# Two perceptron-heavy blocks in fp32: who makes the remainders of the down-projection weights

## The chip, the cores and the metric

One core of a Trainium2 chip runs the whole program. The metric is the device time of one execution in microseconds; the times below are of the kernel before the change.

## The reference

Two transformer blocks run one after the other on one sequence of 512 tokens and width 1024, all in fp32. The first has a recurrent mixer, differential attention, a memory cross-attention and a perceptron; the second has two layers, a gated linear attention and a sliding-window attention, each followed by a perceptron. The three perceptrons all have this form (their weights are 1024 x 4096 and 4096 x 1024):

```python
def sq_relu_mlp(h, w_up, w_down):
    u = jax.nn.relu(h @ w_up)
    return (u * u) @ w_down
```

TensorE gets fp32 accuracy from three products of rounded operands: each weight block w is split into hi = w rounded to the matrix format and lo = w - hi, each activation likewise, and w x is taken as hi x_hi + lo x_hi + hi x_lo.

## The kernel before, in words

Weights stream through in blocks of 1 MB, numbered by n over the whole program. Block n lies in slot n % 4 of `raw` (the SBUF tile that loads fill); SP issues the loads in order (`load_mlp`, L1359), each when `raw_free` says that the slot's last user is done. ScalarE rounds a block into its hi tile (`hi`, L2014, the activation at L2021). For plain blocks VectorE makes the remainder (`lo`, the subtraction at L2399). In the perceptrons lo is written over the raw weights: `raw_lo` and `raw` are two names for the same bytes.

A perceptron has 32 blocks, in an order written out in `mlp_order` (L115): up blocks U(g, b) make two of the 16 chunks of hidden activations, down blocks D(g, b) add a product of four chunks' worth of rows onto half of the output. The order is U(0,0), U(0,1), U(1,0), D(0,0), U(1,1), D(0,1), and then up and down in turn. So i = 0, 1, 2 are up blocks done with plain chunks of 24 matmuls (`chunk`); i = 3 is the first down block; from i = 4 on even i are up blocks done by a scheme of seven block products (`up_fast`, L1597 for its matmuls, 84 of 256 columns each), odd i are down blocks (`down`, 48 matmuls of 512 columns), and i = 30 and 31 are down blocks again. In the third perceptron the last two down blocks are not run by `down` but by `last_chunk`, half the tokens at a time. There are 16 down blocks in each perceptron, 48 in all.

TensorE runs the blocks in that order and waits at the head of each one in `block_ready` for its remainder. ScalarE's order is written out by hand in its `mlp` (L2104): near the head of a perceptron it rounds block n + 3 behind the squares of block n + 1 (`square(n + 1, 1)`), then block n + 5 behind the activations of block n + 2. In the loop over i = 4, 6, .. 28 it takes four snapshots of the running up block out of PSUM (`snap`), rounds the sums of the next up block (`group_hi`) and rounds the down block n + i + 3; then come `square_pair` and `pair_hi`, which square and round the activations just made. At i = 28 it rounds block n + 30 between the first and the second snapshot. VectorE's `mlp` (L2540) calls `lo` for one down block in each turn. GpSimd issues small loads and does additions (`fold_acc`, L1468) between the perceptrons; during them it waits.

`DONE`, `STD_NO` and `FAST` are tables that say which value a semaphore has once a block is done; `wide` views a block as four rows of 512 columns, which is how down blocks are laid out.

Of the kernel before, what the change touches and what calls it, by code (L numbers as in the profile page):

```python
# [19 lines left out]
P = 128  # L20
T = 512
D = 1024
# [22 lines left out]
CONST, _c = {}, 0  # L45
# [64 lines left out]
          ("SOA", 2, 4, (0, 1)), ("SOB", 2, 4, ANY), ("MLP3", 32, 2, WOB_RING)]  # L110
FIRST, ACC, DONE = {}, [], []
FAST, STD_NO, MLP_AT, HI_FREE = {}, [], {}, []


def mlp_order(last):  # L115
# [10 lines left out]
for _name, _count, _chunks, _ring in STAGES:  # L126
    FIRST[_name] = len(ACC)
    for _i in range(_count):
        ACC.append(len(ACC_BANK))
        DONE.append(_done)  # L130
        STD_NO.append(len(ACC) - 1 - len(FAST))
        HI_FREE.append(len(ACC) - 3)
        if _name[:3] == "MLP":
            _n = len(ACC) - 1
            _nth = int(_name[3]) - 1
            _kind, _g, _b = mlp_order(_nth == 2)[_i]
            MLP_AT[_n] = (_nth, _i, _kind, _g, _b)
            HI_FREE[_n] = _n - (2 if _i < 2 else 3)
            if _kind == "U" and _i >= 4:
                FAST[_n] = len(FAST)  # L140
                continue
            _chunks = 4 if _kind == "D" else 2
            if _nth == 2 and _i >= 30:
                continue
        _done += _chunks
        for _c in range(_chunks):
            _k = len(ACC_BANK)
            _b = _ring[_k % len(_ring)]
            ACC_BANK.append(_b)
            ACC_NEED.append(_last.get(_b, 0))  # L150
            _last[_b] = _k + 1
# [2 lines left out]
ACC.append(len(ACC_BANK))  # L154
DONE.append(_done)
STD_NO.append(N_END - len(FAST))


PRODUCTS = dict(P1=(4, 0, 3), P2=(6, 1, 0), P6=(2, 5, 3), P5=(1, 3, 2), P7=(0, 4, 3), P4=(5, 6, 1), P3=(3, 2, 2))
# [71 lines left out]
def program(nc, A, out):  # L231
# [2 lines left out]
    ds = bass.ds  # L234
    ctx = ExitStack()
    with ctx:
        sem_names = """ld_const ld_vec ld_small ld_lora ld_x0 ld_x1 ld_x2 ld_x3 ld_x4 ld_x5 ld_x6 ld_x7 ld_mem ld_kv st_kv0 st_kv1 kv_hi kv_lo ld_gk ld_bias0 ld_bias1 ld_bias2 ld_rel st_bias st_out
            w_hi_ready w_lo_ready acc_done acc_evac vec_ready bias_mm bias_ev ld_w0 half_hi half_lo
            norm_sq norm_add norm_ss norm_ln norm_rstd x_hi x_lo h_final
            fold_sq fold_add fold_ss fold_step  # L240
            mn_sq mn_add mn_step mx_hi mx_lo
# [300 lines left out]
        def rwkv_pe(pe, mm, wait, fill):  # L542
# [54 lines left out]
            for st, hp in RW_OPS["p"]:  # L597
# [9 lines left out]
                if (st, hp) in entry:  # L607
                    wait(*entry[(st, hp)])
                if st == "zw":
                    wait("ld_lora", 48)  # L610
                    wait("rw_lora", 1)
                    last = mm(bank[:], lora[0:64, fs], p_rw[0:64, 12, :], start=True, stop=True)
                elif st == "za":
# [368 lines left out]
        def gla_pe(pe, mm, wait, chunk, blocks, block_tm, norm_stat, chunk_tokens):  # L982
# [3 lines left out]
            mm(X[2][:], C("ones"), fold_acc[:], start=True, stop=True).then_inc(S["fold_ss"], 1)  # L986
            chunk(N_GQK, 0, g_hi, g_lo_)
            wait("acc_evac", ACC[N_GQK])
            wait("ld_gk", 64)
            wait("fold_step", 5)  # L990
            for c in range(4):
                r = slice(32 * c, 32 * c + GLR)
# [336 lines left out]
        def _(sp):  # L1329
            def raw_free(n):  # L1330

                if n >= 4 and n - 4 in FAST:
                    sp.wait_ge(S["st_mm"], 7 * FAST[n - 4] + PRODUCT_NO["P4"])
                elif n >= 4 and n - 4 in MLP_AT:
                    sp.wait_ge(S["acc_done"], DONE[n - 3])
                elif n >= 4:
                    sp.wait_ge(S["w_lo_ready"], STD_NO[n - 4] + 1)

            def load(n, src, cols=BW):

# [76 lines left out]

        @block.gpsimd
        def _(pool):
            for i, name in enumerate(("lam_q1", "lam_q2")):  # L1420
                pool.dma_start(lamv[i:i + 1, 0, :], A[name]).then_inc(S["ld_small"], 16)
            for i, name in enumerate(("lam_k1", "lam_k2")):
# [2 lines left out]
            pool.wait_ge(S["x_lo"], KT)  # L1425
            pool.wait_ge(S["norm_sq"], KT)
            pool.dma_start(memT[:], A["mem"]).then_inc(S["ld_mem"], 16)
            pool.dma_start(lora[0:64, :], A["w_decay_up"][0]).then_inc(S["ld_lora"], 16)
            pool.dma_start(lora[64:128, :], A["a_up"][0]).then_inc(S["ld_lora"], 16)
            pool.dma_start(g_up[:], A["g_up"][0]).then_inc(S["ld_lora"], 16)  # L1430

            pool.wait_ge(S["ld_vec"], 16)
            for k in range(14):
# [21 lines left out]
            pool.dma_start(vf[:].rearrange("p t (b n) -> p (t b) n", b=4), kv_rows[:, 8:16, :]).then_inc(S["ld_kv"], 16)  # L1455
            pool.wait_ge(S["acc_evac"], ACC[N_MQ] + 1)
            pool.wait_ge(S["norm_ss"], 2)
            pool.dma_start(onehot[:], A["onehot"]).then_inc(S["ld_rel"], 16)
            pool.dma_start(relx[0:32, :], A["rel_table_2"]).then_inc(S["ld_rel"], 16)
            pool.dma_start(relx[32:33, :], A["consts"][0:1, CONST["ones"][0]:CONST["ones"][0] + 16]).then_inc(S["ld_rel"], 16)  # L1460
            pool.wait_ge(S["bias_ev"], 1)
            pool.dma_start(bias_rows, biasrow[:].unsqueeze(1).to_broadcast([16, P, 384])).then_inc(S["st_bias"], 16)
            pool.wait_ge(S["st_bias"], 16)
            for c in range(1, KT):
                pool.wait_ge(S["fold_sq"], c + 1)
                if c > 1:
                    pool.wait_ge(S["fold_add"], c - 1)
                nc.gpsimd.tensor_tensor(fold_acc[:], (ut[0] if c == 1 else fold_acc)[:], ut[c % 2][:], ALU.add).then_inc(S["fold_add"], 1)  # L1468
            pool.wait_ge(S["acc_evac"], ACC[N_GLR])
            for c in range(4):  # L1470
                pool.dma_start(w_gk2[32 * c:32 * c + GLR, :], A["a_w_gk2_2"][0][:, c * P:c * P + P]).then_inc(S["ld_gk"], 16)
            pool.wait_ge(S["acc_evac"], ACC[N_KV])
            for c in range(3):
                pool.dma_start(bias[c][:], bias_skewed(c)).then_inc(S[f"ld_bias{c}"], 16)
# [4 lines left out]
            for c in range(KT):  # L1479
                if c + 3 < KT:  # L1480
                    pool.wait_ge(S["sw_s"], 4 * (c + 1))
                    pool.dma_start(bias[c % 3][:], bias_skewed(c + 3)).then_inc(S[f"ld_bias{c % 3}"], 16)
                pool.wait_ge(S["sw_rd"], c + 1)
                r_ = sw_small[c % 2][4]
                s_ = sc[c % 3][:, 0, :, P:256]
                nc.gpsimd.tensor_tensor(s_, s_, r_[:, 0:2].unsqueeze(2).to_broadcast([P, 2, P]), ALU.mult)
                s_ = sc[c % 3][:, 1:4].rearrange("p a b n -> p (a b) n")
                nc.gpsimd.tensor_tensor(s_, s_, r_[:, 2:8].unsqueeze(2).to_broadcast([P, 6, 256]),
                                        ALU.mult).then_inc(S["sw_p"], 1)


        @block.tensor
        def _(pe):
# [9 lines left out]
                return M[ACC_BANK[k]]  # L1503

            def block_ready(n):
                pe.wait_ge(S["w_lo_ready"], STD_NO[n] + 1)

            def exact3(dst, wh, wl, xh, xl, start, stop):
                mm(dst, wh, xh, start=start, stop=False)  # L1509
# [303 lines left out]
            def mem_transposes(hd):  # L1813
                wait("ma_p", hd + 1)
                if hd:
                    wait("ma_pt_lo", 2 * hd)
                else:
                    wait("bias_ev", 1)
                for t in range(2):
                    for qb in range(4):  # L1820
                        last = nc.tensor.transpose(X[2 + t][:, qb * P:qb * P + P], me[hd % 2][:, qb, t * P:t * P + P],
                                                   C("ident"))
                    last.then_inc(S["ma_tr"], 1)
# [19 lines left out]
            chunk(N_MQ + 1, 1, x2_hi, x2_lo)  # L1843
            chunk(N_MQ + 2, 0, x2_hi, x2_lo)
            mem_scores(1)
            wait("ld_rel", 48)
            mm(X[3][0:16, 0:384], relx[:], onehot[:], start=True, stop=True).then_inc(S["bias_mm"], 1)
            chunk(N_MQ + 2, 1, x2_hi, x2_lo)
            mem_transposes(0)
            chunk(N_MQ + 3, 0, x2_hi, x2_lo)  # L1850
# [162 lines left out]
        def _(act):  # L2013
            def hi(n):  # L2014

                slot_free(act, n)
                arrived(act, n)
                if n == N_GLR:
                    nc.scalar.activation(copies(hi_of(n)), copies_of(raw[:, n % 4]), ACT.Copy).then_inc(S["w_hi_ready"], 1)
                else:  # L2020
                    nc.scalar.activation(hi_of(n)[:, :, :], raw[:, n % 4], ACT.Copy).then_inc(S["w_hi_ready"], 1)  # L2021

            def norm_chunk(i, c, src, ready=None, x=None, tok=T, sem=("norm_sq", "norm_add", "x_hi")):

# [253 lines left out]
            hi(N_MQ + 3)  # L2278
            query_hi(4)
            mem_exps(1)  # L2280
            act.wait_ge(S["bias_mm"], 1)
            nc.scalar.activation(biasrow[:], X[3][0:16, 0:384], ACT.Copy).then_inc(S["bias_ev"], 1)
            query_hi(5)
            hi(N_MOA)
            mem_pt_hi(0)
# [104 lines left out]
        def _(dve):  # L2390
# [149 lines left out]
            def mlp(n, nth, rstd_of, i_, j_, fname, foff, wname=None, woff=0, hi_=None, lo_=None):  # L2540
# [37 lines left out]
                up_out(n + 1, 0)  # L2578
                comb_lo(nth, 2)
                up_out(n + 1, 1)  # L2580
                lo(n + 3)
                pair_lo(n + 1)
                comb(nth, 3, fname, foff)
                up_out(n + 2, 0)
# [8 lines left out]
                add(3, 0, 1, 2)  # L2593
                for i in range(4, 30, 2):
                    add(i - 1, 3)
                    lo(n + i + 1)
                    if i < 28:
                        sums(i + 2)
                        group_lo(n + i + 2, 0)
                        group_lo(n + i + 2, 1)  # L2600
                    up_even(n + i)
                    up_odd(n + i)
                    if i < 28:
                        group_lo(n + i + 2, 2)
                        group_lo(n + i + 2, 3)
                    else:
                        lo(n + 30)
                    if nth < 2 or i < 28:
                        if i % 4 == 0:
                            add(i + 1, 0)  # L2610
                        pair_lo(n + i)
                        add(i + 1, *range(1 if i % 4 == 0 else 0, 3))
                if nth == 2:
                    pair_lo(n + 28)
                    lo(n + 31)
                    final(29)
                    norm_step(i_, 3, j_, h[:, 3, :], gain(3), lo_, hi_)
                    return
                add(29, 3)
                lo(n + 31)  # L2620
                final(30)
                lo(n + 32)
                final(31)
# [380 lines left out]
```

## Time and profile before

| | us |
|---|---|
| three runs | 1935.07, 1935.68, 1937.64 |
| median | 1935.68 |
| span of the profiled execution | 1937.4 |
| TensorE busy in it | 1912.2 |
| VectorE busy in it | 1333.0 |
| ScalarE busy in it | 837.4 |
| GpSimd busy in it | 121.1 |

The span runs from the first to the last instruction of one profiled execution. TensorE's matmuls overlap in its pipeline, so the durations in single rows are longer than the distance from one matmul's start to the next one's; the distance is what a stream of them costs. PE is TensorE, PEld its weight loads, DVE is VectorE, ACT ScalarE, POOL GpSimd, SP the engine that issues most loads.

### The profile page before, as it was taken

Reading aid. Unit: us, or ns where it says so; the run is one execution under the profiler, and the core shown is the slowest. Engines: PE = TensorE matmul, PEld = TensorE weight load, DVE = VectorE, ACT = ScalarE, POOL = GpSimd, SP = SyncE. Lnnn points to the kernel's source line nnn. Section 1 sums busy time; section 2 is a strip of 40 time slices with the busy share of each in tenths; the row PEclk is TensorE's granted clock in tenths of the full one; section 3 lists DMA queues with packets and bytes.
Section 4 is the critical chain, followed back from the end, with each engine's and each line's share of the span. In section 5 each row is a group of like instructions: output and inputs, shape, how many; then the busy total and the mean of one; then the engine's idle time right before and its main releaser. Section 6 shows DMA issues by size and latency. Waiting matters only on the chain.

```text
span 1937.4 us, 32713 instructions
## 1 busy us (share of the span) xinstructions
PE 1912.2 (99%) x14002; PEld 1646.6 (85%) x14002; DVE 1333.0 (69%) x1755; ACT 837.4 (43%) x1254; POOL 121.1 (6%) x130
## 2 busy tenths in 40 slices
PE   8999999999999999999999999999999999999998
PEld 6877898888788898887989889889987788898897
DVE  5576869576677777767545687767677768777665
ACT  4333744344354344344224443434444645344342
POOL 1055100000000000010000000000002300000000
PEclk9999999999999999999999999999999999999999
DMA  8221402237123233224220233323342113233231
GB/s 271 88 66 66 137 10 80 88 132 128 46 89 108 87 110 109 88 78 140 90 87 23 66 98 98 109 87 109 102 144 88 50 47 106 90 106 109 87 109 44
DMA packets 138831, 182.62 MB, mean 94 GB/s; under 512 B 4917, under 2 KB 103429, under 8 KB 138304
## 3 DMA queue, kind: packets, MB, share of 16 engines
q1 hardware_dynamic: 135392, 168.91, 26.9%
q0 software_dynamic: 3296, 11.63, 2.9%
q8 instruction: 111, 1.82, 0.4%
q14 instruction: 32, 0.26, 0.0%
HBM read 172.66 MB, written 7.34 MB: 93 GB/s over the span
## 4 chain that ended last, share of the span: by engine, by line
PE 94%; DVE 3%; ACT 1%; issue 1%; DMA 0%; SPq 0%; DVEq 0%; ACTq 0%
PE X L1597 20%; PE M L1509 19%; PE M L1510 19%; PE M L1511 19%; PE X L643 3%; PE M L1570 1%; PE M L1571 1%; PE M L1572 1%; PE M L1925 1%; PE X L1902 1%; PE X L1913 1%; PE X L1780 1%; PE X L1749 1%; DMA raw<-in_w_in_dram 0%; PE X L1511 0%
## 5 line engine op out<-in xcount | busy, mean ns | idle before, releaser
L1510 PE MATMUL M<-u,raw_lo 128*128 128x512 f32 x728 | 287.9, 396 | 0.0
L1509 PE MATMUL M<-u,w_hi 128*128 128x512 f32 x728 | 287.9, 395 | 0.0
L1511 PE MATMUL M<-u,w_hi 128*128 128x512 f32 x728 | 286.1, 393 | 0.0
L2021 ACT ACTIVATE w_hi<-raw 128x2048 fp32r<-128x2048 f32 x113 | 215.6, 1908 | 93.5 <-PE M L1511 47.9
L2076 ACT ACTIVATE us<-X 128x256 f32<-128x256 f32 x156 | 60.2, 386 | 426.9 <-PE X L1597 426.9
L2549 DVE TENSOR_TENSOR h<-h,M 128x512 f32<-128x512 f32 x184 | 123.7, 685 | 144.7 <-PE M L1511 144.6
L1597 PE MATMUL X<-t,w_hi 128*128 128x256 f32 x936 | 173.2, 282 | 0.0
L1511 PEld LDWEIGHTS M<-u,w_hi 128*128 128x128 f32 x728 | 137.6, 189 | 32.8
L1509 PEld LDWEIGHTS M<-u,w_hi 128*128 128x128 f32 x728 | 136.8, 188 | 30.8
L1510 PEld LDWEIGHTS M<-u,raw_lo 128*128 128x128 f32 x728 | 136.7, 188 | 29.8
L2399 DVE TENSOR_TENSOR raw_lo<-raw,w_hi 128x2048 fp32r<-128x2048 f32 x57 | 130.3, 2287 | 23.7 <-ACT w_hi L2021 23.7
L1597 PEld LDWEIGHTS X<-t,w_hi 128*128 128x128 f32 x936 | 146.4, 188 | 0.0
L2399 DVE TENSOR_TENSOR w_lo<-raw,w_hi 128x2048 fp32r<-128x2048 f32 x52 | 118.9, 2289 | 29.9 <-ACT w_hi L2021 29.9
L1597 PE MATMUL X<-t,w_lo 128*128 128x256 f32 x468 | 131.7, 281 | 0.0
L1597 PE MATMUL X<-f,wx 128*128 128x256 f32 x624 | 117.8, 282 | 0.0
L1597 PEld LDWEIGHTS X<-f,wx 128*128 128x128 f32 x624 | 98.6, 189 | 1.7
L2480 DVE TENSOR_TENSOR w_lo<-w_sum,w_hi 128x1024 fp32r<-128x1024 f32 x78 | 91.9, 1220 | 0.0
L1597 PEld LDWEIGHTS X<-t,w_lo 128*128 128x128 f32 x468 | 88.2, 188 | 0.0
L1597 PE MATMUL X<-f,raw_lo 128*128 128x256 f32 x312 | 87.9, 282 | 0.0
L1509 PE MATMUL M<-gx_hi,w_hi 128*128 128x512 f32 (+2 forms) x232 | 85.1, 367 | 1.0 <-DVE w_lo L2399 0.5
L1511 PE MATMUL M<-gx_lo,w_hi 128*128 128x512 f32 (+2 forms) x232 | 84.3, 363 | 0.0
L1510 PE MATMUL M<-gx_hi,w_lo 128*128 128x512 f32 (+2 forms) x232 | 84.3, 363 | 0.0
(525 smaller groups left out, 4542.2 us busy)
## 6 DMA issues: line engine op xcount, KB each, us to landing
raw<-in_w_up_dram SPq DMA_DIRECT2D x48, 1024.0 KB, 5.4
raw<-in_w_down_dram SPq DMA_DIRECT2D x48, 1024.0 KB, 5.0
raw<-in_w_in_dram SPq DMA_DIRECT2D x12, 1024.0 KB, 8.6
raw<-in_a_w_in_dram SPq DMA_DIRECT2D x12, 1024.0 KB, 5.3
h<-in_x_dram SPq DMA_DIRECT2D x16, 256.0 KB, 4.8
raw<-in_w_mk_dram SPq DMA_DIRECT2D x4, 1024.0 KB, 4.9
raw<-in_w_mv_dram SPq DMA_DIRECT2D x4, 1024.0 KB, 5.2
raw<-in_w_out_dram SPq DMA_DIRECT2D x4, 1024.0 KB, 5.1
```

The lines of the kernel that those rows point to most:

```text
L643: last = mm(blk(bank, hh, cp, cpar), a_, b_, start=True, stop=True)
L1509: mm(dst, wh, xh, start=start, stop=False)
L1510: mm(dst, wl, xh, start=False, stop=False)
L1511: return mm(dst, wh, xl, start=False, stop=stop)
L1570: mm(o_, hi[:, kt, ts_], w_hi[:, n % 2, kt, cs], start=kt == 0, stop=False)
L1571: mm(o_, hi[:, kt, ts_], w_lo[:, n % 2, kt, cs], start=False, stop=False)
L1597: last = mm(region(r), (wl if p_ == 1 else wh)[:, m, :], xl if p_ == 2 else xh, start=name in ("P1", "P2", "P4", "P5") and m == 0 and p_ = ...
L2021: nc.scalar.activation(hi_of(n)[:, :, :], raw[:, n % 4], ACT.Copy).then_inc(S["w_hi_ready"], 1)
L2076: nc.scalar.activation(at_, region(r), ACT.Copy).then_inc(S["st_snap"], 1)
L2399: TTO(lo_of(n)[:, :, :], raw[:, n % 4], hi_of(n)[:, :, :].bitcast(f32), ALU.subtract).then_inc(S["w_lo_ready"], 1)
L2480: TTO(to_, from_, hi_.bitcast(f32), ALU.subtract).then_inc(S["st_lo"], 1)
L2549: TTO(h[:, 4 * b + c, :], h[:, 4 * b + c, :], acc(n + i, c), ALU.add).then_inc(S["acc_evac"], 1)
```

## The change

The down blocks' remainders are made without VectorE. ScalarE rounds the block into its hi tile as before and then writes the negated rounded weights over the raw ones (`raw_lo` = -hi, in place). GpSimd waits for that and issues a transfer that reads the same raw weights once more from memory and adds them onto what lies there: -hi + w = lo. TensorE waits at the head of a down block for this transfer's semaphore (two, taken in turn) instead of VectorE's. VectorE's 16 calls of `lo` for down blocks are gone from each perceptron; `LO_NO` numbers the remainders that VectorE still makes. GpSimd's transfers of a perceptron are three loops: for the first one behind the store of the bias table, for the second behind the four loads of `w_gk2`, for the third at the end of its program. Some semaphores for small tables are merged to make room for the new names.

```diff
+DOWN, LO_NO = {}, []
...
+        LO_NO.append(STD_NO[-1] - len(DOWN))
...
+            if _kind == "D":
+                DOWN[_n] = len(DOWN)
...
                 elif n >= 4:
-                    sp.wait_ge(S["w_lo_ready"], STD_NO[n - 4] + 1)
+                    sp.wait_ge(S["w_lo_ready"], LO_NO[n - 4] + 1)
...
+            def remainders(first):
+
+                _, down = mlps[first]
+                for n in range(first, first + 32):
+                    if n in DOWN:
+                        k, (_, _, _, g, b) = DOWN[n], MLP_AT[n]
+                        pool.wait_ge(S["down_neg"], k + 1)
+                        if k >= 2:
+                            pool.wait_ge(S["acc_done"], DONE[DOWN_AT[k - 2]] + 1)
+                        pool.dma_start(wide(raw_lo[:, n % 4]), down[:, 4 * g:4 * g + 4, 512 * b:512 * b + 512],
+                                       accum_op=ALU.add).then_inc(S[f"down_lo{k % 2}"], 16)
...
             pool.wait_ge(S["st_bias"], 16)
+            remainders(N_MLP1)
             for c in range(1, KT):
                 pool.wait_ge(S["fold_sq"], c + 1)
...
+            remainders(N_MLP2)
             pool.wait_ge(S["acc_evac"], ACC[N_KV])
...
+            remainders(N_MLP3)
...
             def block_ready(n):
-                pe.wait_ge(S["w_lo_ready"], STD_NO[n] + 1)
+                if n in DOWN:
+                    wait(f"down_lo{DOWN[n] % 2}", 16 * (DOWN[n] // 2 + 1))
+                else:
+                    wait("w_lo_ready", LO_NO[n] + 1)
...
                     nc.scalar.activation(hi_of(n)[:, :, :], raw[:, n % 4], ACT.Copy).then_inc(S["w_hi_ready"], 1)
+                if n in DOWN:
+                    nc.scalar.activation(raw_lo[:, n % 4], raw[:, n % 4], ACT.Copy, scale=-1.0).then_inc(S["down_neg"], 1)
...
                 up_out(n + 1, 1)
-                lo(n + 3)
                 pair_lo(n + 1)
...
                 for i in range(4, 30, 2):
                     add(i - 1, 3)
-                    lo(n + i + 1)
...
-                    else:
-                        lo(n + 30)
...
-                    lo(n + 31)
```

## Rows read from the trace of the kernel before

**Rows 1.** The page: busy time by engine, and the chain that ended last, by engine.
```profile
PE 1912.2 (99%) x14002; PEld 1646.6 (85%) x14002; DVE 1333.0 (69%) x1755; ACT 837.4 (43%) x1254; POOL 121.1 (6%) x130
...
PE 94%; DVE 3%; ACT 1%; issue 1%; DMA 0%; SPq 0%; DVEq 0%; ACTq 0%
```

**Rows 2.** Busy time by stretch (us, engines, granted clock, DMA): middle of perceptron one.
```profile
571.00:835.00 264.00, 264.00 (x1669) 238.38 (x1668) 189.89 (x213) 108.62 (x138) 0.00 (x0) 1.00 0.31 100
```

**Rows 3.** Waits of TensorE's weight loads: us in total, times, longest.
```profile
PEld M L1509 <- DVE w_lo L2399: 1.7, 2, 1.0
```

**Rows 4.** Line 2399, VectorE's remainders: count, ns min/median/max, first and last start.
```profile
L2399 DVE TENSOR_TENSOR raw_lo<-raw,w_hi x57: 2284/2285/2294, 518.4 to 1899.4; 128x2048 fp32r<-128x2048 f32 x57
```

**Rows 5.** Timeline of ScalarE (start us, us): rounding of each first down block.
```profile
554.28 1.90 ACT L2021 ACTIVATE w_hi<-raw 128x2048 fp32r<-128x2048 f32 x1
...
1120.93 1.90 ACT L2021 ACTIVATE w_hi<-raw 128x2048 fp32r<-128x2048 f32 x1
...
1612.77 1.90 ACT L2021 ACTIVATE w_hi<-raw 128x2048 fp32r<-128x2048 f32 x1
```

**Rows 6.** Perceptron three, i = 28: ScalarE's timeline; chain: TensorE's seven products.
```profile
1885.37 1.91 ACT L2021 ACTIVATE w_hi<-raw 128x2048 fp32r<-128x2048 f32 x1
...
1883.56 10.01 PE X L1597 x84
```

**Rows 7.** Timeline of TensorE: first matmuls of the three first down blocks.
```profile
559.85 0.40 PE L1509 MATMUL M<-u,w_hi 128*128 128x512 f32 x1
560.09 0.40 PE L1510 MATMUL M<-u,raw_lo 128*128 128x512 f32 x1
...
1126.90 0.40 PE L1509 MATMUL M<-u,w_hi 128*128 128x512 f32 x1
...
1618.29 0.40 PE L1509 MATMUL M<-u,w_hi 128*128 128x512 f32 x1
```

**Rows 8.** Timelines: rounding and first matmul of i = 13 and i = 5.
```profile
645.45 1.91 ACT L2021 ACTIVATE w_hi<-raw 128x2048 fp32r<-128x2048 f32 x1
...
665.60 0.39 PE L1509 MATMUL M<-u,w_hi 128*128 128x512 f32 x1
...
569.58 1.90 ACT L2021 ACTIVATE w_hi<-raw 128x2048 fp32r<-128x2048 f32 x1
...
581.01 0.40 PE L1509 MATMUL M<-u,w_hi 128*128 128x512 f32 x1
```

**Rows 9.** Timelines: rounding and first use of the very last down block.
```profile
1897.50 1.90 ACT L2021 ACTIVATE w_hi<-raw 128x2048 fp32r<-128x2048 f32 x1
...
1906.01 0.28 PE L1509 MATMUL X<-u,w_hi 128*128 128x256 f32 x1
```

**Rows 10.** Timelines of GpSimd and SP; transfers (KB each, median us to landing).
```profile
388.05 0.55 POOL L1454 DMA_DIRECT2D kf_mem<-kv_rows  x1 [77.03 <-DVE p_rw L979]
388.59 0.55 POOL L1455 DMA_DIRECT2D vf_mem<-kv_rows  x1
...
391.10 0.37 SPq L1342 DMA_DIRECT2D raw<-in_w_mq_dram  x1
...
kf_mem<-kv_rows POOLq DMA_DIRECT2D x1, 1024.0 KB, 5.2
vf_mem<-kv_rows POOLq DMA_DIRECT2D x1, 1024.0 KB, 7.2
...
bias_rows<-biasrow POOLq DMA_DIRECT2D x1, 3072.0 KB, 33.3
```

**Rows 11.** Timeline of SP at perceptron one's first down block.
```profile
560.04 0.37 SPq L1342 DMA_DIRECT2D raw<-in_w_up_dram  x1
```

**Rows 12.** TensorE's first and eleventh matmul; last stretch by engine and granted clock.
```profile
7.87 0.76 PE L1509 MATMUL M<-xm_hi,w_hi 128*128 128x512 f32 x1 [7.87 <-DVE xm_lo L2638]
...
12.28 0.49 PE L1510 MATMUL M<-xm_hi,w_lo 128*128 128x512 f32 x1
...
1932.00:1937.00 5.00, 0.00 (x0) 0.00 (x0) 2.57 (x7) 0.00 (x0) 0.00 (x0) 0.50 0.63 210
```

More of the change, by code:

```diff
@@ L156 @@
 STD_NO.append(N_END - len(FAST))
+LO_NO.append(STD_NO[-1] - len(DOWN))
+DOWN_AT = list(DOWN)
 PRODUCTS = dict(P1=(4, 0, 3), P2=(6, 1, 0), P6=(2, 5, 3), P5=(1, 3, 2), P7=(0, 4, 3), P4=(5, 6, 1), P3=(3, 2, 2))
@@ L236, in program @@
     with ctx:
-        sem_names = """ld_const ld_vec ld_small ld_lora ld_x0 ld_x1 ld_x2 ld_x3 ld_x4 ld_x5 ld_x6 ld_x7 ld_mem ld_kv st_kv0 st_kv1 kv_hi kv_lo ld_gk ld_bias0 ld_bias1 ld_bias2 ld_rel st_bias st_out
-            w_hi_ready w_lo_ready acc_done acc_evac vec_ready bias_mm bias_ev ld_w0 half_hi half_lo
+        sem_names = """ld_const ld_vec ld_small ld_tables ld_x0 ld_x1 ld_x2 ld_x3 ld_x4 ld_x5 ld_x6 ld_x7 ld_mem ld_kv st_kv0 st_kv1 kv_hi kv_lo down_neg down_lo0 down_lo1 ld_bias0 ld_bias1 ld_bias2 st_bias st_out
+            w_hi_ready w_lo_ready acc_done acc_evac vec_ready bias_step ld_w0 half_hi half_lo
             norm_sq norm_add norm_ss norm_ln norm_rstd x_hi x_lo h_final
@@ L609, in rwkv_pe @@
                 if st == "zw":
-                    wait("ld_lora", 48)
+                    wait("ld_tables", 48)
                     wait("rw_lora", 1)
@@ L988, in gla_pe @@
             wait("acc_evac", ACC[N_GQK])
-            wait("ld_gk", 64)
+            wait("ld_tables", 160)
             wait("fold_step", 5)
@@ L1427, in _ @@
             pool.dma_start(memT[:], A["mem"]).then_inc(S["ld_mem"], 16)
-            pool.dma_start(lora[0:64, :], A["w_decay_up"][0]).then_inc(S["ld_lora"], 16)
-            pool.dma_start(lora[64:128, :], A["a_up"][0]).then_inc(S["ld_lora"], 16)
-            pool.dma_start(g_up[:], A["g_up"][0]).then_inc(S["ld_lora"], 16)
+            pool.dma_start(lora[0:64, :], A["w_decay_up"][0]).then_inc(S["ld_tables"], 16)
+            pool.dma_start(lora[64:128, :], A["a_up"][0]).then_inc(S["ld_tables"], 16)
+            pool.dma_start(g_up[:], A["g_up"][0]).then_inc(S["ld_tables"], 16)
             pool.wait_ge(S["ld_vec"], 16)
@@ L1457, in _ @@
             pool.wait_ge(S["norm_ss"], 2)
[L1458 to L1461, printed above, removed]
+            pool.dma_start(onehot[:], A["onehot"]).then_inc(S["ld_tables"], 16)
+            pool.dma_start(relx[0:32, :], A["rel_table_2"]).then_inc(S["ld_tables"], 16)
+            pool.dma_start(relx[32:33, :], A["consts"][0:1, CONST["ones"][0]:CONST["ones"][0] + 16]).then_inc(S["ld_tables"], 16)
+            pool.wait_ge(S["bias_step"], 2)
             pool.dma_start(bias_rows, biasrow[:].unsqueeze(1).to_broadcast([16, P, 384])).then_inc(S["st_bias"], 16)
             pool.wait_ge(S["st_bias"], 16)
+            remainders(N_MLP1)
             for c in range(1, KT):
@@ L1470, in _ @@
             for c in range(4):
-                pool.dma_start(w_gk2[32 * c:32 * c + GLR, :], A["a_w_gk2_2"][0][:, c * P:c * P + P]).then_inc(S["ld_gk"], 16)
+                pool.dma_start(w_gk2[32 * c:32 * c + GLR, :], A["a_w_gk2_2"][0][:, c * P:c * P + P]).then_inc(S["ld_tables"], 16)
+            remainders(N_MLP2)
             pool.wait_ge(S["acc_evac"], ACC[N_KV])
@@ L1817, in mem_transposes @@
                 else:
-                    wait("bias_ev", 1)
+                    wait("bias_step", 2)
                 for t in range(2):
@@ L1845, in _ @@
             mem_scores(1)
-            wait("ld_rel", 48)
-            mm(X[3][0:16, 0:384], relx[:], onehot[:], start=True, stop=True).then_inc(S["bias_mm"], 1)
+            wait("ld_tables", 96)
+            mm(X[3][0:16, 0:384], relx[:], onehot[:], start=True, stop=True).then_inc(S["bias_step"], 1)
             chunk(N_MQ + 2, 1, x2_hi, x2_lo)
@@ L2280, in _ @@
             mem_exps(1)
-            act.wait_ge(S["bias_mm"], 1)
-            nc.scalar.activation(biasrow[:], X[3][0:16, 0:384], ACT.Copy).then_inc(S["bias_ev"], 1)
+            act.wait_ge(S["bias_step"], 1)
+            nc.scalar.activation(biasrow[:], X[3][0:16, 0:384], ACT.Copy).then_inc(S["bias_step"], 1)
             query_hi(5)
@@ L2619, in mlp @@
                 add(29, 3)
-                lo(n + 31)
                 final(30)
```

## The prediction

> **What bounds the kernel now.** I read the page first: busy time by engine and the chain that ended last. TensorE is busy for 1912.2 us of a span of 1937.4 us, and 94% of the chain is TensorE work; VectorE, which the change relieves, is busy for 69% [rows 1]. Then the table by stretches, for the middle of a perceptron, where most of the removed work lies: TensorE is busy for 264.00 of 264 us there, at a granted clock of 1.00 [rows 2]. Then the waits: in the whole execution TensorE's weight loads wait 1.7 us, twice, for the line that makes remainders, and the tile named there is w_lo, which no perceptron's down block uses [rows 3]. So VectorE's subtraction of a down block costs TensorE nothing today. It is off the path, and taking it away can give nothing back by itself. What remains is to see whether the new way to the same tile is ready in time at each of the 48 down blocks. For that I read the timeline of ScalarE and of TensorE round the first, a middle and the last down block of a perceptron, and the GpSimd transfers for a price.
>
> **What is removed.** 48 subtractions of 2.285 us [rows 4], 109.7 us of VectorE time, all beside a busy TensorE: gain 0 (at most the 1.7 us of waits above, and those belong to other blocks). VectorE's next steps (pair_lo, comb, add) come up to 2.3 us earlier; TensorE waits for none of them, so nothing follows. The renamed and merged semaphores wait for the same events: 0.
>
> **What is added on ScalarE.** Behind each down block's rounding stands a second copy of the same size, taken as 1.9 us like the rounding [rows 5]; 48 of them are 91 us on an engine that is busy for 43% [rows 1]. Queued behind it are square_pair and pair_hi (the squared activations), which come 1.9 us later. In the middle of a perceptron their user is a whole block away: free. At i = 28 the new copy stands ahead of the snapshots: the rounding begins at 1885.37 and takes 1.91, so the copy ends at about 1889.1 and the snapshot behind it some 0.4 later, at 1889.5 (my estimate, from its 256 columns against the rounding's 2048 and a fixed part); the fifth of that block's seven products, which waits for this snapshot, would start at 1883.56 + 4/7 of 10.01 = 1889.3 [rows 6]. With hand-offs 0.4 us each, 1.2 us for three perceptrons (between 0 and 1.9 each).
>
> **What is added on GpSimd and the queues.** 48 transfers of 1 MB. GpSimd has nothing else queued behind them that anyone needs before a perceptron ends: the fold additions come after its last block, the bias loads later still. The down block's weights are read from memory a second time. The new path of one block is: rounding, negated copy, transfer, and only at its landing may TensorE begin the block. Call the time from the end of the negated copy to TensorE's start L. What counts is how long each block already has to wait anyway, its allowance.
>
> First down block (i = 3): ScalarE's rounding starts at 554.28, 1120.93 and 1612.77 [rows 5], because it stands behind the squares of the second up block. The negated copy ends 3.72 us later (the next activation starts some 0.1 before the last one ends): 558.00, 1124.65 and 1616.49. TensorE starts the block at 559.85, 1126.90 and 1618.29 [rows 7]. The allowances are 1.85, 2.25 and 1.80, 5.9 us together.
>
> Middle blocks: rounding from 645.45, copy done at 649.2, block due at 665.60 [rows 8]: 16.4 us. The blocks at i = 5 have 581.01 - 573.3 = 7.7 us [rows 8], and more by whatever the first one stalls, since TensorE waits while ScalarE goes on. The blocks at i = 30 and 31 of the first two perceptrons have at least the down block ahead of them as cover.
>
> Last block of the third perceptron: rounding from 1897.50, copy done at 1901.2; its weights are first used at 1906.01 [rows 9]: allowance 4.8 us.
>
> **The size of L.** No accumulating transfer is in this trace. The nearest rows are two plain GpSimd loads of 1 MB. The first landed after 5.2 us; the second, issued 0.54 later, after 7.2, so that 2 MB took 388.05 to 395.79, 7.7 us, with a load from SP joining 3.05 us behind the first issue [rows 10]. A transfer that adds must fetch the raw weights and the negated copy, so I count 1 MB of sum as 2 MB of plain traffic: 7.7. At the first down block SP's next load is issued at 560.04 [rows 11], 2 us behind instead of 3: half of that microsecond more, and 0.1 for two hand-offs: L = 8.3 there. Behind the last block nothing is loaded: 7.7. The lower bound is the plain megabyte, 5.2, if the second operand is free. The upper bound from rows is the slowest GpSimd transfer, 3 MB in 33.3 us [rows 10], 11.1 per MB, with the same additions 11.7. I take 8.3, because adding has the traffic of the two loads and not the memory-side writes of the slow one.
>
> The Trainium skill weighs in on this from both sides. Its page "DMA: Bandwidth & Descriptors", section on the anatomy of a GpSimd DMA, gives about 2.0 us plus bytes over 436 GB/s; counted on the 1 MB that lands that is an estimate of 4.4 us, and the first blocks would stall 3 x 4.4 - 5.9 = 7.3 us together, a total near 1943. Its page "Collectives: The Full Stack", section on the bandwidth ceiling, says that an add in the DMA path needs two source reads and so runs at about half the rate; the same formula on 2 MB is 6.8 us, 14.5 us of stall. By the first rule the time would be rival 1, or just under it. The trace has 5.2 for a plain megabyte, above the formula's 4.4, and no accumulating transfer to decide between the two.
>
> **The clock.** A stall of this kind is longer than any that TensorE has in the perceptrons now. At the start of the execution ten matmuls of 512 columns took from 7.87 to 12.28, 4.41 us at the lower level (1.2 GHz), where the same ten at full clock take 10 x 0.24 = 2.4 (559.85 to 560.09 is one) [rows 7, 12]. At the end, with TensorE idle, the granted clock is 0.50 [rows 12]. So after 6 us without work I expect the lower clock, and one such return costs 2.0 us. The Trainium skill, "TensorE: Matmul & The Clock Gate", Part 1, says the same: the throttled state is the default and activity releases it.
>
> **Sum.** First blocks: 3 x 8.3 - 5.9 = 19.0. Last block: 7.7 - 4.8 = 2.9. Snapshots: 1.2. Clock after the three long stalls: 6.0. Together 29.1 us, nothing against it. The profiled span of 1937.4 lies within the runs' 1935.07 to 1937.64, so the difference goes on the median: 1935.7 + 29.1 = 1964.8, forecast 1965.
>
> **Rivals.**
> 1. Cheap addition: L = 5.3 and the clock holds. 3 x 5.3 - 5.9 + 0.5 = 10.5: 1946. For it: the plain row. Against it: the second operand has to come through the same 16 engines.
> 2. Dear addition, L from 11.7 up to the middle blocks' allowance of 16.4. At 16.4: 43.3 + 11.6 + 1.2 + four clock returns of 2.0 = 64: 2000. For it: the arithmetic may be slower than the traffic.
> 3. Beyond that point every middle block stalls too. At L = 20: first blocks 54.1, last 12.3, 36 middle blocks of 3.6 are 130, with clock 8 and more: about 2140.
> 4. The other side, not slower: VectorE's load is what shapes the seams, and the transfer lands inside the allowance. Its place is the first down block, its price is at most the 1.7 us of waits on remainders [rows 3], 1934.0, and it decides at L below 1.9 us. Against it stands every GpSimd row: none moves a megabyte in under 5.2.
> That the change does not do what it says would be an addition done in other pieces than one transfer; that is case 2 or 3.
>
> **How the numbers follow.** Forecast case (L about 6 to 11.7, 1950 to 1981) 0.68; cheap 0.08; dear 0.12; beyond 0.09; other side 0.03. The range reaches from the cheap case to the point where the middle blocks begin to stall, 1946 to 2000. A measurement of this kernel can tell about 0.2%, 3.9 us, from no change. All cases but the last lie above that: slower 0.97, same 0.02, faster 0.01.
>
> **What would show it.** In the changed profile TensorE should have a gap just ahead of the down block that follows the third up block, three times, of 6 to 7 us, ended by a GpSimd transfer, and one of about 3 us some 30 us before the end; granted clock under 1.00 right behind the long ones; no gap at middle blocks; VectorE's busy time down by some 110 us and ScalarE's up by some 91. Landing times near 8 us settle L. I am wrong if the gaps are there but short (L is mis-sized low), if middle blocks have gaps (L above 16), or if TensorE's time grows without gaps, which would be contention that I have priced at nothing.

## The result

The changed kernel takes 1973.24 us (median; 1970.47 to 1974.13) beside 1936.66 for the kernel before in the same comparison (1935.07 to 1938.55): ratio 1.0189, 95% interval 1.0175 to 1.0204. The forecast was 1965 in a range of 1946 to 2000. It is 36.6 us slower where 29.1 were worked out.

The page of the changed kernel, busy time and chain, to be held against [rows 1]:

```profile
span 1968.7 us, 32807 instructions
PE 1918.7 (97%) x14002; PEld 1650.9 (84%) x14002; DVE 1227.1 (62%) x1707; ACT 923.8 (47%) x1302; POOL 183.0 (9%) x178
...
PE 74%; issue 18%; DVE 4%; DMA 2%; ACT 2%; POOL 0%; DVEq 0%; POOLq 0%; ACTq 0%
```

VectorE lost 106 us of work, ScalarE got 86 more and GpSimd 62, and the same 14002 matmuls take longer. The chain's 18% of "issue" (time for which the profile names no releaser) is not TensorE's: followed back from a late transfer, the chain runs along GpSimd's queue, and two of its pieces are 316 us of that time, GpSimd's waits for ScalarE's copy ahead of the second and the third perceptron's first transfer (the chain in order of time: start us, us, what):

```profile
880.66 249.76 issue
1130.44 9.05 DMA raw_lo<-in_w_down_dram
...
1565.76 66.13 issue
1631.91 9.59 DMA raw_lo<-in_w_down_dram
```

The waits of TensorE say where the time went (us in total, times, longest):

```profile
PE M L1533 <- DMA raw_lo<-in_w_down_dram: 22.8, 3, 8.0
...
PE X L1533 <- DMA raw_lo<-in_w_down_dram: 4.1, 1, 4.1
...
PE X L1621 <- issue: 0.5, 3, 0.2
```

Four waits for the new transfers in the whole program: three of 7 to 8 us, one of 4.1. (L1533 is the line that was L1509; L1621 was L1597.) The last line is three short waits within the seven products at i = 28, for which the profile names no releaser; they come back below. The first of the four waits in the timelines of ScalarE, GpSimd and TensorE, with the transfers of that stretch (last column: us from issue to landing), against [rows 5, 7, 11]:

```profile
549.41 1.90 ACT L2045 ACTIVATE w_hi<-raw 128x2048 fp32r<-128x2048 f32 x1
551.21 1.90 ACT L2047 ACTIVATE raw_lo<-raw 128x2048 fp32r<-128x2048 f32 x1
...
553.70 1.35 POOL L1435 DMA_DIRECT2D raw_lo<-in_w_down_dram  x1 [110.64 <-ACT raw_lo L2047]
...
554.74 0.39 PE L1535 MATMUL M<-f,w_hi 128*128 128x512 f32 x1
563.03 0.80 PE L1533 MATMUL M<-u,w_hi 128*128 128x512 f32 x1 [7.90 <-DMA raw_lo<-in_w_down_dram]
563.62 0.63 PE L1534 MATMUL M<-u,raw_lo 128*128 128x512 f32 x1
...
raw_lo<-in_w_down_dram POOLq DMA_DIRECT2D x1, 1024.0 KB, 9.3
raw<-in_w_up_dram SPq DMA_DIRECT2D x1, 1024.0 KB, 10.1
```

The chain reads off line by line: rounding, negated copy until 553.11, 0.59 us until GpSimd issues, 9.3 us until the sum has landed, TensorE at 563.03. The matmuls behind it follow each other at more than 0.4 us. The busy table by stretches (the column after POOL is the granted clock) shows why, and that the middle of the perceptron [rows 2] is as full as it was:

```profile
563.00:567.00 4.00, 3.97 (x9) 3.14 (x10) 3.32 (x4) 3.97 (x4) 0.00 (x0) 0.50 0.43 150
567.00:571.00 4.00, 4.00 (x19) 3.22 (x18) 2.75 (x4) 1.96 (x2) 1.30 (x1) 1.00 0.00 0
1139.50:1143.50 4.00, 3.97 (x9) 3.14 (x10) 3.32 (x4) 3.97 (x5) 0.00 (x0) 0.50 0.46 159
1641.50:1645.50 4.00, 3.96 (x9) 3.13 (x10) 3.32 (x4) 3.97 (x4) 0.00 (x0) 0.50 0.33 114
...
571.00:835.00 264.00, 264.00 (x1649) 237.40 (x1648) 157.20 (x195) 129.53 (x147) 15.38 (x12) 1.00 0.61 152
```

Both kernels issue the same matmuls in the same order, so the start of each one in one trace can be taken from its start in the other. For example, the last matmul ahead of the first down block starts at 554.74 in the changed kernel and at 559.62 in the kernel before,

```profile
559.62 0.40 PE L1511 MATMUL M<-f,w_hi 128*128 128x512 f32 x1
```

and the block's own first matmul at 563.03 and 559.85 [rows 7]: the difference goes from -4.88 to 3.18, a gap of 8.06. From here on the difference moves only in a few places, and these steps are the account of the loss:

| place | us |
|---|---|
| gaps ahead of the three first down blocks: 8.06, 7.11, 8.14 | 23.31 |
| lower clock behind them: 1.90, 2.04, 1.90 | 5.84 |
| gap ahead of the very last down block | 4.31 |
| lower clock behind that | 1.48 |
| i = 28, snapshots: 0.41 in each perceptron | 1.23 |
| sum | 36.17 |

The very last block in the timelines of ScalarE, GpSimd and TensorE, and TensorE's busy table behind it, against [rows 9]:

```profile
1924.97 1.90 ACT L2047 ACTIVATE raw_lo<-raw 128x2048 fp32r<-128x2048 f32 x1
...
1927.44 1.28 POOL L1435 DMA_DIRECT2D raw_lo<-in_w_down_dram  x1 [11.44 <-ACT raw_lo L2047]
...
1931.55 0.29 PE L1535 MATMUL X<-u,w_hi 128*128 128x256 f32 x1
1935.99 0.58 PE L1533 MATMUL X<-u,w_hi 128*128 128x256 f32 x1 [4.15 <-DMA raw_lo<-in_w_down_dram]
...
1936.00:1939.00 3.00, 3.00 (x14) 3.00 (x15) 0.05 (x1) 0.00 (x0) 0.00 (x0) 0.50 0.00 0
```

And the seven products at i = 28 in the third perceptron: one piece of 10.01 us in the chain before [rows 6], now split behind the fourth product, 10.42 us from the first start to the last end:

```profile
1908.83 5.71 PE X L1621 x48
1914.71 4.54 PE X L1621 x36
```

The medians differ by 36.6. The two profiled executions differ by 31.3 alone, because the one of before stood 4.9 us later when its first perceptron's down blocks began, a part of the program in which none of the new transfers runs; in the traces of the six kernels below it stands 1.0 to 2.4 us later. A run's time is some 1.8 us above its span (1970.47 to 1968.7 here), so the profiled execution of before, with its span of 1937.4, was one of the longer ones and not, as the prediction had it, in the middle of the runs; the sum was a difference put on the median, and that step isn't touched.

### The profile page after: what moved, and what is told of

It is laid out like the page before. It is cut to its first block, busy times and chain, and to the rows that moved or that the text cites. A ratio compares the mean times of both kernels' runs of the same rounds, so it can differ in the third digit from the quotient of the medians.

```text
span 1968.7 us, 32807 instructions
## 1 busy us (share of the span) xinstructions
PE 1918.7 (97%) x14002; PEld 1650.9 (84%) x14002; DVE 1227.1 (62%) x1707; ACT 923.8 (47%) x1302; POOL 183.0 (9%) x178
## 4 chain that ended last, share of the span: by engine, by line
PE 74%; issue 18%; DVE 4%; DMA 2%; ACT 2%; POOL 0%; DVEq 0%; POOLq 0%; ACTq 0%
PE X L1621 20%; PE M L1533 14%; PE M L1534 14%; PE M L1535 14%; PE X L649 3%; DMA raw_lo<-in_w_down_dram 2%; PE X L1926 1%; PE X L1804 1%; PE X L1773 1%; PE M L1949 0%; ACT w_hi L2045 0%; PE X L1937 0%; PE X L1533 0%; PE M L1594 0%; PE M L1596 0%
## 5 line engine op out<-in xcount | busy, mean ns | idle before, releaser
L1533 PE MATMUL M<-u,w_hi 128*128 128x512 f32 x728 | 290.6, 399 | 22.8 <-DMA raw_lo<-in_w_down_dram 22.8
L1533 PEld LDWEIGHTS M<-u,w_hi 128*128 128x128 f32 x728 | 138.3, 190 | 55.2 <-DMA raw_lo<-in_w_down_dram 24.1
L1435 POOL DMA_DIRECT2D raw_lo<-in_w_down_dram x48 | 61.7, 1286 | 1253.5 <-ACT raw_lo L2047 1231.7
L1621 PE MATMUL X<-t,w_hi 128*128 128x256 f32 x936 | 174.0, 282 | 0.5 <-issue 0.5
L1621 PEld LDWEIGHTS X<-t,w_hi 128*128 128x128 f32 x936 | 146.7, 188 | 1.1 <-issue 1.1
L2521 DVE SCALAR_TENSOR_TENSOR us<-us,X 128x512 f32<-128x512 f32 x39 | 26.9, 689 | 169.2 <-ACT us L2102 169.2
L1621 PE MATMUL X<-t,w_lo 128*128 128x256 f32 x468 | 131.8, 282 | 0.0
L1621 PE MATMUL X<-f,wx 128*128 128x256 f32 x624 | 117.8, 282 | 0.0
L1621 PEld LDWEIGHTS X<-f,wx 128*128 128x128 f32 x624 | 98.6, 189 | 1.7
L2540 DVE TENSOR_TENSOR u<-us,u 128x1024 fp32r<-128x1024 f32 x47 | 57.4, 1222 | 63.4 <-ACT u L2123 63.4
L2047 ACT ACTIVATE raw_lo<-raw 128x2048 fp32r<-128x2048 f32 x48 | 91.4, 1905 | 0.0
L1621 PEld LDWEIGHTS X<-t,w_lo 128*128 128x128 f32 x468 | 88.2, 188 | 0.0
L1621 PE MATMUL X<-f,raw_lo 128*128 128x256 f32 x312 | 87.9, 282 | 0.0
```

The source lines that it names most:

```text
L1435: pool.dma_start(wide(raw_lo[:, n % 4]), down[:, 4 * g:4 * g + 4, 512 * b:512 * b + 512], accum_op=ALU.add).then_inc(S[f"down_lo{k % 2}"], 16)
L1621: last = mm(region(r), (wl if p_ == 1 else wh)[:, m, :], xl if p_ == 2 else xh, start=name in ("P1", "P2", "P4", "P5") and m == 0 and p_ = ...
L2047: nc.scalar.activation(raw_lo[:, n % 4], raw[:, n % 4], ACT.Copy, scale=-1.0).then_inc(S["down_neg"], 1)
```

## The experiments

The theory: the loss sits where the time from the end of the negated copy to TensorE's start (L) is longer than what a block has to wait anyway, that is at four blocks of 48, with the clock's cost on top; the other transfers and VectorE's relief are worth nothing. The rivals: the loss is spread over all blocks by contention; VectorE's relief buys something that the gaps hide; the slow matmuls have another cause than the gap.

### Only the first down blocks back to VectorE

```diff
-            if _kind == "D":
+            if _kind == "D" and _i != 3:
...
                 up_out(n + 1, 1)
+                lo(n + 3)
                 pair_lo(n + 1)
```

> Only the first down block of each perceptron (i = 3) gets its remainder from VectorE again; the other 45 blocks keep the transfer. Theory (the loss sits in the short allowance of the first down blocks and of the very last block): the three gaps of 8.2, 7.2 and 8.2 us and their three stretches at the lower clock, 1.9 us each, are gone, 29.3 us in all; what is left over before is the last block's 4.4 + 1.5 and the snapshots' 1.3, 7.2 us: 1936.7 + 7.2 = 1943.9. Rival (48 extra megabytes and the second copy cost something at every block, by contention): at least half of the 36.6 us stays, 1955 or more. Granted clock 1.00 behind the three first blocks by the theory.

Measured: 1947.07 us, ratio 1.0054 (1.0039 to 1.0069). That is 26 us back for three blocks of 48, so the loss isn't spread; but 3 us are missing. The waits of TensorE have them:

```profile
PE X L1533 <- DMA raw_lo<-in_w_down_dram: 3.9, 1, 3.9
PE M L1533 <- DMA raw_lo<-in_w_down_dram: 3.1, 3, 1.2
```

There are three new waits, and the timelines of TensorE and ScalarE in the first perceptron tell which block they belong to [rows 8]:

```profile
580.84 0.50 PE L1533 MATMUL M<-u,w_hi 128*128 128x512 f32 x1 [1.18 <-DMA raw_lo<-in_w_down_dram]
...
569.90 1.91 ACT L2047 ACTIVATE raw_lo<-raw 128x2048 fp32r<-128x2048 f32 x1
```

It is i = 5. Its copy ends at 571.81 and TensorE starts 9.0 us later, where 7.7 had been at hand. As long as i = 3 stalls, i = 5 gains the length of that stall and is in time; once the first gap is closed, the second opens: 1.43, 1.09 and 1.35 us in the three perceptrons. With the last block's 4.1 and its clock's 2.5, and 1.2 for the snapshots, the steps between the traces add up to 11.7 from the start of the perceptrons; the medians differ by 10.1 (the profiled execution, 1949.14, is the longest of the four). Behind the three first blocks the granted clock is 1.00, as the theory had it.

### All transfers kept, the first block rounded earlier

```diff
                 hi(n + 2)
                 pair_hi(n)
+                hi(n + 3)
...
                 square(n + 1, 1)
-                hi(n + 3)
                 pair_hi(n + 1)
```

> All 48 transfers stay; ScalarE rounds and negates the first down block (i = 3) behind the activations of the first up block instead of behind the squares of the second, some 9 us earlier, since its weights have long arrived and ScalarE is idle there. Theory: the allowance goes from 1.85 to about 11.0 us and the transfer needs 10.0 from the end of the copy, so the three gaps and their clock are gone: 1943.9 as with the remainder made by VectorE. Rival 1 (the transfer is stretched when it starts beside SP's next load, at 548.9 in the old timeline): gaps of 1 to 2 us stay, 1945 to 1950. Rival 2 (bulk contention): 1955 or more.

Measured: 1948.02 us, ratio 1.0058 (1.0043 to 1.0073): an order of ScalarE's instructions alone gives 25 of the 36.6 us back. Timelines of ScalarE, SP, GpSimd and TensorE at the first block, and its transfer:

```profile
544.88 1.90 ACT L2047 ACTIVATE raw_lo<-raw 128x2048 fp32r<-128x2048 f32 x1
...
547.10 0.37 SPq L1373 DMA_DIRECT2D raw<-in_w_down_dram  x1
...
547.36 1.35 POOL L1435 DMA_DIRECT2D raw_lo<-in_w_down_dram  x1 [101.26 <-ACT raw_lo L2047]
...
558.63 0.51 PE L1533 MATMUL M<-u,w_hi 128*128 128x512 f32 x1 [0.47 <-DMA raw_lo<-in_w_down_dram]
...
raw_lo<-in_w_down_dram POOLq DMA_DIRECT2D x1, 1024.0 KB, 11.2
```

The first block's transfer in the second and in the third perceptron:

```profile
raw_lo<-in_w_down_dram POOLq DMA_DIRECT2D x1, 1024.0 KB, 11.8
raw_lo<-in_w_down_dram POOLq DMA_DIRECT2D x1, 1024.0 KB, 11.1
```

The theory's 1943.9 is missed, and the time lies in the range of this run's first rival. What that rival names is seen as well: SP's load is issued within 0.4 us of the transfer (0.26 ahead of it here), and the sum lands after 11.1 to 11.8 us, where the changed kernel, with SP's load 1.5 to 2.2 us behind, has 9.1 to 9.6. The steps at the first blocks are smaller than that rival put them, 0.7, 0.7 and 0.3 us where the gaps were 7 to 8. The rest of the 11 us is in the places of the run before: i = 5 (0.2 and, in the third perceptron, 1.3), the snapshots (1.2), the last block (4.3, and 2.2 for its clock).

### The transfer without its addition

```diff
-                        pool.dma_start(wide(raw_lo[:, n % 4]), down[:, 4 * g:4 * g + 4, 512 * b:512 * b + 512],
-                                       accum_op=ALU.add).then_inc(S[f"down_lo{k % 2}"], 16)
+                        pool.dma_start(wide(raw_lo[:, n % 4]), down[:, 4 * g:4 * g + 4, 512 * b:512 * b + 512]).then_inc(S[f"down_lo{k % 2}"], 16)
```

> The transfers overwrite instead of add (the remainder is then wrong: the raw weights stand in its place, so the added part of the computation is left out); everything else as in the changed kernel. If a second operand is what makes the transfer slow: landing falls from 8.6 to about 6 us (a plain megabyte took 5.2 on this queue, and issuing 512 pieces takes 0.7 us longer than 128), the first blocks' gaps fall by some 2.6 each with the clock cost unchanged, and the last block's gap to 1.8: about 1973.2 - 7.8 - 2.6 - 1.5 = 1961. If the issue, the pieces and the cast set it and adding is free: landing 8 to 8.6 and 1970 to 1973.

Measured: 1958.43 us, ratio 1.0112 (1.0097 to 1.0127). The changed kernel first, its transfers in the list of DMA issues (median us to landing) and their issuing on GpSimd in the groups by line (busy us, mean ns of one, then idle time):

```profile
raw_lo<-in_w_down_dram POOLq DMA_DIRECT2D x48, 1024.0 KB, 8.6
...
L1435 POOL DMA_DIRECT2D raw_lo<-in_w_down_dram x48 | 61.7, 1286 | 1253.5 <-ACT raw_lo L2047 1231.7
```

The same two lines of the kernel without the addition:

```profile
raw_lo<-in_w_down_dram POOLq DMA_DIRECT2D x48, 1024.0 KB, 5.5
...
L1435 POOL DMA_DIRECT2D raw_lo<-in_w_down_dram x48 | 35.8, 746 | 1265.6 <-ACT raw_lo L2046 1243.4 <-PE M L1534 22.2
```

Adding costs 3.1 us a transfer, 0.54 of it in the issuing. So the plain megabyte [rows 10] was about the right price for the part that isn't the addition, and the addition isn't free. The gaps of the first blocks fall to 4.2 to 4.4 us, the last one to 1.1; the time is 2.6 us under the 1961 that a landing of 6 us would have given. The Trainium skill ("DMA: Bandwidth & Descriptors", anatomy of a GpSimd DMA, with the two source reads of "Collectives: The Full Stack") gave estimates of 4.4 without and 6.8 with the second read; the runs measure 5.5 and 8.6. Both are longer than the estimates, but what the addition costs as a ratio, 1.56, agrees with the 1.55 of those estimates. Part of that agreement is luck: the surplus itself is 3.1 us where the estimates give 2.4, and 0.54 of it is issuing. In the Trainium skill ("Collectives: The Full Stack", the bandwidth ceiling) the two source reads are those of a ReduceScatter between cores; whether a second read, the arithmetic or something else makes this transfer slower, no run here tells.

### The opposite selection

```diff
-            if _kind == "D":
+            if _kind == "D" and (_i == 3 or _nth == 2 and _i == 31):
...
+                    lo(n + i + 1)
...
+                        lo(n + 30)
...
+                lo(n + 31)
```

> The opposite selection: only four blocks take the transfer, the first down block of each perceptron and the very last block; VectorE makes the other 44 remainders. Theory: all the loss but the snapshots' 1.3 us is in these four: 1936.7 + 35.3 = 1972. Rival (the loss is spread over the blocks): four of 48 keep a small part of it, under 1945. In between would mean that both carry some.

Measured: 1972.99 us, ratio 1.0186 (1.0169 to 1.0203), as slow as with all 48. Busy time by engine:

```profile
PE 1921.0 (97%) x14002; PEld 1652.9 (84%) x14002; DVE 1325.2 (67%) x1751; ACT 845.5 (43%) x1258; POOL 126.6 (6%) x134
```

VectorE is back at 1325 us of work and only four blocks use the transfer, and the loss is there: the steps from the first perceptron's down blocks on come to 34.7 us where the changed kernel has 36.2. The steps at i = 28 are gone, since no copy stands ahead of those snapshots here. The other 44 transfers carry none of the loss that these runs can tell.

### Only covered transfers

```diff
-            if _kind == "D":
+            if _kind == "D" and _i not in (3, 5) and (_nth, _i) != (2, 31):
...
-                        hi(n + 30)
+                        hi(n + 30, later=True)
                     for k in range(1, 4):
+                        if i == 28 and k == 3:
+                            negated(n + 30)
                         snap(n + i, k)
```

with VectorE's `lo` for those seven blocks put back; `negated` is the second copy as a step of its own.

> Transfers only where the traces so far show cover: VectorE again makes the remainders of i = 3 and i = 5 of each perceptron and of the very last block (7 of 48), and at i = 28 the negated copy of block 30 stands behind the third snapshot instead of ahead of the second. Theory (41 covered transfers and 94 us less of VectorE are worth nothing either way, since TensorE is the bound): the time of the kernel before, 1936.9, ratio within 0.2% of 1; TensorE's starts keep a shift of under 0.5 us against the kernel before over each perceptron. Rival 1 (VectorE's relief buys something that the gaps hid): 1930 to 1933. Rival 2 (the extra 41 MB and the second copies cost by contention, or i = 7 is late in its turn): 1940 to 1945.

Measured: 1936.82 us beside 1937.01, ratio 0.9998 (0.9989 to 1.0007). Page and middle stretches (columns as in [rows 2]):

```profile
PE 1911.6 (99%) x14002; PEld 1646.6 (85%) x14002; DVE 1240.4 (64%) x1714; ACT 910.5 (47%) x1295; POOL 173.9 (9%) x171
...
571.00:835.00 264.00, 264.00 (x1663) 238.09 (x1663) 162.78 (x202) 132.89 (x151) 16.75 (x13) 1.00 0.59 149
1140.00:1400.00 260.00, 260.00 (x1637) 234.40 (x1636) 158.48 (x195) 129.47 (x147) 16.65 (x13) 1.00 0.58 148
```

VectorE has 93 us less to do than before and the DMA engines are almost twice as busy in the middle of a perceptron (0.59 against 0.31), and neither moves the time. Within each of the three perceptrons the shift against the kernel before stays within 0.1 us, so the steps at i = 28 are gone too, with the copy behind the third snapshot. This is the same time as the kernel before, not better; no version here beats it.

### Work in the place of the gap

```diff
                     if kind == "D":
+                        for q in range(30 if i == 3 else 0):
+                            mm(X[0][:, 0:T], f_hi[:, 0, 0:P], f_hi[:, q % KT, :], start=True, stop=True)
                         down(n + i, nth, i, g, b)
```

> The changed kernel with 30 matmuls of 512 columns, whose result nobody reads, put on TensorE ahead of each first down block's wait: 7.0 us of work in the place of 7 to 8 us of idleness; the real work and the waits stay as they are. If the lower clock behind the gaps comes from TensorE's idleness and costs 1.9 us each: granted clock 1.00 behind the first blocks, and 1973.2 - 5.7 = 1967.5. If the slow matmuls behind the gaps came from something else that happens there (the transfer that has just landed, SP's load beside it): they stay and the time is 1973. If the fill delays the block itself: above 1973.

Measured: 1968.51 us, ratio 1.0159 (1.0145 to 1.0173), 4.7 us under the changed kernel. Timeline of TensorE at the first block, and its busy table (granted clock after POOL):

```profile
557.49 6.96 PE L1678 MATMUL X<-f 128*128 128x512 f32 x30
565.64 0.50 PE L1533 MATMUL M<-u,w_hi 128*128 128x512 f32 x1 [1.19 <-DMA raw_lo<-in_w_down_dram]
565.98 0.39 PE L1534 MATMUL M<-u,raw_lo 128*128 128x512 f32 x1
...
565.60:569.60 4.00, 3.96 (x17) 3.24 (x18) 3.31 (x4) 3.97 (x5) 0.00 (x0) 1.00 0.39 136
```

The block still starts when its transfer has landed, and the matmuls behind it run at the full clock: 17 of them in 4 us where the changed kernel had 9; in the second and third perceptron the granted clock is 1.00 there as well. The transfer and SP's load beside it are the same (landing 9.4 and 10.1 us), so the slow matmuls came from TensorE's idleness and not from what happened beside it. The last block has no filling: behind its wait of 4.4 us the granted clock is 0.50, as in the changed kernel. Of the clock's 5.8 us, 4.8 come back in the traces, mostly because the three blocks start 0.8 us later in all.

## Why the prediction was right, and where its sizes were off

- **VectorE's relief is worth nothing: right, shown** by the run with covered transfers only. 109.7 us were priced at 0; the ratio is 0.9998.
- **The places: right.** First block of each perceptron, last block of the third, the snapshots at i = 28, none in the middle. The runs with the opposite selection and with the first blocks given back show the first two. The snapshots' 1.2 us, as forecast, are too little for a time; in the traces the step is there in every kernel with a copy ahead of the second snapshot and gone in the two without.
- **The size of L at the first blocks: the step that was mis-sized.** 8.3 was taken, 9.9, 9.4 and 9.9 came out (each gap and its allowance), so 23.3 us in place of 19.0. The step counted 1 MB of sum as two plain loads of 7.7 us. The landings were 9.3, 9.1 and 9.6; in the first, issuing 512 pieces with an addition is 1.35 where the plain load's row had 0.55, and the hand-off from ScalarE's copy to GpSimd's issue, put at 0.05, is 0.59 there (0.3 at the other two and at most blocks). The half microsecond for SP's nearer load fits the difference to the median landing of 8.6; that the load is its cause is argued, from the longer landings with a still nearer load in the run with the earlier rounding. The direction of the choice between the bounds was right: an addition lies between the plain 5.2 and the 11.7.
- **The last block: the same step.** 7.7 was taken, the copy's end at 1926.87 and TensorE's start at 1935.99 make it 9.1: gap 4.3 in place of 2.9. No weights were loaded beside it, and its transfer landed after 8.5.
- **The clock: right, with one return missing.** Three of 2.0 us were counted, three of 1.9 to 2.0 came, and a fourth of 1.5 behind the last block, whose gap I had thought short enough to leave it out. That the gap is the cause is shown by the run with work in its place. The size of a return varies: behind the same last gap it is 2.5 and 2.2 us in the first two experiments.
- **The allowance of i = 5: right as it stood** (no gap while i = 3 stalls), and the run that gave i = 3 back shows the other half of that sentence: 7.7 us are less than the 9.0 that L is there.
- **The rivals.** The cheap addition (1946) is refuted by the run without addition, 5.5 against 8.6 us to land. The dear one, from 11.7 up, and the one beyond the middle blocks' 16.4 us did not come. The rival on the other side is refuted by the run with covered transfers. In the rival beyond, the last block's stall at L = 20 is 20 - 4.8 = 15.2 and not 12.3; its total is 3 us higher, and nothing else hangs on it.
- **The range** of 1946 to 2000 was wide, from one plain load to the middle blocks' allowance, so that the time lies inside it says less than that the gaps stand where they were forecast.

With these L (29.2 at the three first blocks, 9.1 at the last) and four returns of the clock the same sum gives 29.2 - 5.9 + 4.3 + 1.2 + 7.3 = 36.1, the measured 36.6 within the scatter. The sizes are read from the changed trace, so this shows that no place is missing, not that the sizes could be foretold.

## What to carry to other kernels

Before work is moved off an engine that isn't the bound, ask what the new path's latency is and hold it against the allowance of each use, the first and the last of a loop apart: a path five times as long (some 12 us from the end of the rounding to the finished tile instead of 2.3) was free at 41 of 48 places, once one copy had been moved behind a snapshot, and cost 35 us at four. When a gap is closed, look for the use that the gap had covered, as i = 5 here. And price a gap on TensorE at its length plus the clock's return, here 1.5 to 2.5 us each.

## What the runs showed of the hardware that was not expected

- A GpSimd transfer that adds 1 MB onto SBUF lands 8.6 us after its issue (median; 11.1 to 11.8 in the three cases above where a load from SP was issued within 0.4 us of it), the same transfer without the addition 5.5.
- Adding makes the issuing longer too: 1286 against 746 ns for the same pieces.
- From the end of ScalarE's copy to GpSimd's issue it takes 0.3 us at most blocks and up to 0.66 where nothing else holds GpSimd, where I had put 0.05. At i = 31 of the first two perceptrons it takes 4.0, because there GpSimd still waits for TensorE's work on the down block two before; the first of these sums still landed 5.7 us before its block.
- Behind every wait of TensorE for one of these transfers of 3.8 to 8.0 us the granted clock was 0.50, and that cost 1.5 to 2.5 us a time; behind waits of up to 1.2 us, as in the run with the filling, it stayed at 1.00.
